# Recurrence of an RWKV-7 layer: head norms as 64x64 products, joined with other TensorE work, in a new order

## The reference, cut to what matters

```python
kk = heads(k * k_k)
kk = kk / jnp.maximum(jnp.sqrt(jnp.sum(kk * kk, axis=-1, keepdims=True)), 1e-12)
k = k * (1.0 + (a - 1.0) * k_a)
b_h = kk * a_h
def step(S, inp):
    r_t, w_t, k_t, v_t, na_t, b_t = inp
    sa = jnp.einsum('bhvk,bhk->bhv', S, na_t)
    S = S * w_t[:, :, None, :] + sa[..., None] * b_t[:, :, None, :] + v_t[..., None] * k_t[:, :, None, :]
    return S, jnp.einsum('bhvk,bhk->bhv', S, r_t)
...
mean = jnp.mean(out, axis=-1, keepdims=True)
var = jnp.mean(jnp.square(out - mean), axis=-1, keepdims=True)
out = ((out - mean) * lax.rsqrt(var + LNX_EPS)).reshape(B, T, D) * lnx_w + lnx_b
```

## Time and profile before

| | |
|---|---|
| median of 3 runs | 3540.37 us (3538.47 to 3543.31) |
| the profiled execution | 3546.33 us, its span 3544.6 us |
| granted TensorE clock, mean | 0.987 of full |
| TensorE busy | 3381.6 us of the span |
| VectorE, ScalarE, GpSimd busy | 1652.6, 1354.5, 1740.5 us |
| the recurrence, first product of decays to last of the states | 415.2 to 1126.4 us |

### The profile page before, as it was taken

The page is one execution under the profiler, slowest core; times in us unless marked ns, Lnnn a source line. Parts: engine busy times, 40 slices in busy tenths (PEclk is TensorE's granted clock), DMA queues, the critical chain, the costliest instruction groups (busy, mean ns, idle before and its releaser), DMA issues. The chain is left out here.

```text
span 3544.6 us, 87445 instructions
## 1 busy us (share of the span) xinstructions
PE 3381.6 (95%) x33525; PEld 2940.6 (83%) x33525; DVE 1652.6 (47%) x3032; ACT 1354.5 (38%) x2917; POOL 1740.5 (49%) x1622
## 2 busy tenths in 40 slices
PE   8999889998898999999999999999989999999999
PEld 8999778777777998888888887777769988888887
DVE  7113356555554374444444533333343744444444
ACT  6212445554443133333333434444453333333335
POOL 4434266666654445454554544344433354545455
PEclk9999899999999999999999999999999999999999
DMA  4422211111114011111111234444442111111111
GB/s 154 154 88 89 71 35 36 43 41 38 38 44 143 10 45 46 48 44 45 44 46 47 87 85 96 114 102 91 107 108 66 41 46 47 43 50 42 47 44 73
DMA packets 432743, 233.86 MB, mean 66 GB/s; under 512 B 190979, under 2 KB 417043, under 8 KB 431558
## 3 DMA queue, kind: packets, MB, share of 16 engines
q1 hardware_dynamic: 428882, 215.40, 21.9%
q10 hardware_dynamic: 3572, 14.33, 1.0%
HBM read 187.69 MB, written 47.21 MB: 66 GB/s over the span
## 5 line engine op out<-in xcount | busy, mean ns | idle before, releaser
L2688 DVE TENSOR_TENSOR H<-ps,H 128x512 f32<-128x512 f32 x608 | 419.6, 690 | 463.3 <-PE ps L2351 462.5
L2239 POOL TENSOR_TENSOR split<-work,split 128x512 fp32r<-128x512 f32 x280 | 379.8, 1361 | 493.9 <-ACT split L2510 486.8
L2351 PE MATMUL ps<-split,split 128*128 128x512 f32 x1824 | 514.0, 390 | 0.0
L2404 PE MATMUL ps<-xs,split 128*128 128x512 f32 x1920 | 512.5, 393 | 0.0
L1341 PE MATMUL ps<-arena 64*64 64x64 f32 (+1 forms) x9984 | 400.9, 225 | 37.9 <-issue 21.2
L1341 PEld LDWEIGHTS ps<-arena 64*64 64x64 f32 x9984 | 351.6, 135 | 71.4 <-issue 45.6
L2404 PEld LDWEIGHTS ps<-xs,split 128*128 128x128 f32 x1920 | 349.9, 188 | 68.2
L2351 PEld LDWEIGHTS ps<-split,split 128*128 128x128 f32 x1824 | 339.8, 188 | 70.9 <-DVE H L2688 0.7
L2404 PE MATMUL ps<-split,split 128*128 128x512 f32 x1440 | 366.1, 390 | 0.5 <-issue 0.5
L3278 PE MATMUL ps<-xs,split 128*128 128x384 f32 x1656 | 361.4, 355 | 2.6 <-POOL split L3192 2.6
L601 PE MATMUL ps<-mixed,wsplit_mix 128*128 128x384 f32 x1872 | 331.7, 339 | 7.6 <-DVE mixed L824 7.6
(11 more groups left out here) (325 smaller groups left out, 5972.4 us busy)
## 6 DMA issues: line engine op xcount, KB each, us to landing
work<-in_ffn_w_gu SPq DMA_DIRECT2D x168, 256.0 KB, 2.9
work<-in_ffn_w_down SPq DMA_DIRECT2D x168, 128.0 KB, 2.3
work<-in_cache_v SPq DMA_DIRECT2D x64, 256.0 KB, 3.9
work<-in_cache_k SPq DMA_DIRECT2D x256, 64.0 KB, 2.2
rkv_scratch<-lora ACTq DMA_DIRECT2D x24, 576.0 KB, 2.8
stage_mix<-in_rwkv_w_rkv SPq DMA_DIRECT2D x24, 512.0 KB, 3.8
work<-in_attn_w_qkv SPq DMA_DIRECT2D x24, 512.0 KB, 4.2
h_scratch<-H SPq DMA_DIRECT2D x2, 4608.0 KB, 12.5
```

The source lines that it names most:

```text
L2239: pool.tensor_tensor(w[1], frm, w[0].bitcast(F32), ALU.subtract).then_inc(u_lo, 1)
L2351: last = pe.matmul(full(DOWN + j % 2), w[part][:, (m % 2) * P:(m % 2 + 1) * P], mem.hid[xpart][:, SEG[h]], start=(a == 0), stop=(a == 2))
L2404: last = pe.matmul(full(to), unit(i)[part][:, k * P:(k + 1) * P], operand[xpart][:, k, :], start=(first and k == 0 and a == 0), stop=(k == ...
L2688: dve.tensor_tensor(at, full(DOWN + j % 2), at, ALU.add).then_inc(added, 1)
```

## The change

- `sums` and `expanded` are made of crossed 64x64 products: for each third (6 blocks of 64 columns) six `cross` calls, the sums with 16 columns of ones, the turned roots with the identity. `ksum` and `vsum` are now three items a pair instead of one, each with a turn of the piece bank, and VectorE thresholds each third; the reciprocal and the root still come once, after the third.
- `joined` gets a third case, "under": a piece of a norm next to a fold, or next to a first half of the inverse, is merged with it.
- `FIRST` and the first use of `PATTERN` are replaced by `START` (248 letters for the same items with the new thirds), and `PATTERN` is new (165 letters).
- In the last pair the thirds of `vsum` have their own banks.

```diff
-FIRST = (
-    "CCCCCCCCCCCCCCCCCCCCBBBCCCBCCCCBCCEBECBBEBCBCECFFBCFCCFCCFEBFCFCEBCCFCCCBEBEBFCECCFECFECCCE")
+START = (
+    "CCCCCCCCCCCCCCCCCCCCCCCCBBBCCBCCBECECBCEBBECEBFCCFCFCECFCFBBECCCEFCCEBFBAEFCCCCEECFBCCFAEAEFACCBEBAFBAAECFACAF"
+    "EBFBAECFCAEBFACECAFEBFBEAFACAEBCCBEACAABFBAECAFCCAAECACCBFCECFCACECAFEAEBFEACECCFCAFEBAECAEBFAECAFBECFBAAEACBF"
+    "AACAECAAFAEAABEAFCAAEAFECCAE")
 PATTERN = (
-    "EBADFBAEDABEAFDFEADAFBAEFAAECDADADBFECAFEACFBEBCFAEDAECCAABFAEADAECAFCEADABFCEABECACFAEACEAAEFCAFCAEECABABFAAA"
-    "EFACBEACAFBECCAACFACEBBFCAAEAFCEBBECAAEFCEAFEACFCCE")
+    "DEFADAAEFDAEDAFDEADACBFEBAFEDBADFADEBDAECBEACBEAFCCABEACFAAEAAFECAAEBFACCEBDFAECACFBCEAFACAEFACDAFECAECACBFBAF"
+    "EAEAAACEBABFEAAECCCFAAAECBFEBFCEAAABEAFBACEFACCEFCACECC")
...
+NORMS = ("ksum", "kexp", "vsum", "affine")
...
             out[-1] = ("beside", before[1], (before, key))
+        elif before and before[0] in NORMS and (key[0] == "fold" or key[0] == "invert" and key[2][2] == 0):
+            out[-1] = ("under", key[1], (key, before))
+        elif before and key[0] in NORMS and (before[0] == "fold" or before[0] == "invert" and before[2][2] == 0):
+            out[-1] = ("under", before[1], (before, key))
...
-    for o in range(PAIRS):
-        threads = {"A": serial_items(o) if o + 1 < PAIRS else last_serial_items(), "D": finish_items(o - 1) if o else []}
+    assert not rest.pop("A")
+    for o in range(1, PAIRS):
+        threads = {"A": serial_items(o) if o + 1 < PAIRS else last_serial_items(), "D": finish_items(o - 1)}
...
+            def sums(pb, squares, c, j):
+                return cross(pb[:, TS * j:TS * j + TS], squares[:, c * CW + 64 * j:c * CW + 64 * j + 64], mem.ones[:, 0:TS])
+
+            def expanded(pb, roots, c, j):
+                return cross(pb[:, 64 * j:64 * j + 64], roots[:, c * CW + 64 * j:c * CW + 64 * j + 64], None)
...
+                elif what == "under":
+                    (turn, _, inner), (norm, np, c) = arg
+                    g = inner if turn == "fold" else inner[0]
+                    G = GROUPS[g][1]
+                    if turn == "fold":
+                        fold_start(pr, g)
+                    else:
+                        level_start(pr, g, inner[1])
+                    norm_start(norm, np, c)
+                    for q in range(G):
+                        last = fold_part(g, q) if turn == "fold" else square(pr, g, inner[1], q)
+                        for j in range(6 * q // G, 6 * (q + 1) // G):
+                            norm_part(norm, np, c, j)
+                    last.then_inc(folded[LINE[g]] if turn == "fold" else m1_done[LINE[g]], 1)
...
                 elif what == "ksum":
-                    dve.tensor_scalar(roots(0), head_sums(pb), 1e-24, None, ALU.max).then_inc(piece_free[b], 1)
-                    dve.wait_ge(piece_free[b], n + 1)
-                    dve.reciprocal(m.rs[:, 0, :], m.rs[:, 0, :]).then_inc(kinv, 1)
+                    dve.tensor_scalar(roots(0, arg), head_sums(pb), 1e-24, None, ALU.max).then_inc(piece_free[b], 1)
+                    if arg == 2:
+                        dve.wait_ge(piece_free[b], n + 1)
+                        dve.reciprocal(m.rs[:, 0, :], m.rs[:, 0, :]).then_inc(kinv, 1)
```

More of the change, by code:

```diff
@@ L998, in prepare_items @@
         out += [("w", o, c), ("a", o, c), ("scan", o, c)]
-    out += [("ksum", o, None)] + [("decays", o, c) for c in range(3)]
+    out += [("ksum", o, c) for c in range(3)] + [("decays", o, c) for c in range(3)]
     out += [("kexp", o, c) for c in range(3)] + [("k2", o, None), ("b", o, None)] + [("write", o, g) for g in range(NG)]
@@ L1060, in recurrence_order @@
     for_tensor = list(out)
-    for c, after in enumerate((("vsum", o, None), ("affine", o, 2), ("nst", o, 0))):
+    for c, after in enumerate((("vsum", o, 2), ("affine", o, 2), ("nst", o, 0))):
         for_tensor.remove(("gate", o, c))
@@ L1348, in cross, with norm_start, norm_part @@
                 return last
[L1350 to L1361, removed]
+            def sums(pb, squares, c, j):
+                return cross(pb[:, TS * j:TS * j + TS], squares[:, c * CW + 64 * j:c * CW + 64 * j + 64], mem.ones[:, 0:TS])
+            def expanded(pb, roots, c, j):
+                return cross(pb[:, 64 * j:64 * j + 64], roots[:, c * CW + 64 * j:c * CW + 64 * j + 64], None)
+            def norm_start(what, pr, c):
+                b, n = PIECE_OF[what, pr, c]
+                if n:
+                    pe.wait_ge(piece_free[b], n)
+                if what == "ksum":
+                    pe.wait_ge(kq_ready, pr + 1)
+                elif what == "kexp":
+                    pe.wait_ge(kroot, pr + 1)
+                elif what == "vsum":
+                    cb, cn = PIECE_OF["center", pr, c]
+                    pe.wait_ge(piece_free[cb], cn + 1)
+                else:
+                    pe.wait_ge(vroot, pr + 1)
+            def norm_part(what, pr, c, j):
+                b, n = PIECE_OF[what, pr, c]
+                pb = bank[:, PIECE_BANKS[b], :]
+                if what in ("ksum", "vsum"):
+                    last = sums(pb, m.k2 if what == "ksum" else m.post1, c, j)
+                else:
+                    last = expanded(pb, m.kkn if what == "kexp" else m.post1, c, j)
+                if j == 5:
+                    last.then_inc(piece_done[b], 1)
             def state_values(n):
@@ L1463, in _ @@
                 e = pr % 2
-                if what in PIECES:
+                if what in PIECES and what not in ("ksum", "kexp", "vsum", "affine"):
                     b, n = PIECE_OF[key]
@@ L1474, in _ @@
                     last.then_inc(piece_done[b], 1)
[L1475 to L1478, removed]
-                    pe.wait_ge(kroot, pr + 1)
-                    expanded(pb, m.kkn, arg).then_inc(piece_done[b], 1)
+                elif what in ("ksum", "kexp", "vsum", "affine"):
+                    norm_start(what, pr, arg)
+                    for j in range(6):
+                        norm_part(what, pr, arg, j)
                 elif what == "rk":
@@ L1490, in _ @@
                     cross(pb[:, 0:CW], m.center, third(m.out, arg)).then_inc(piece_done[b], 1)
-                elif what == "vsum":
-                    for c in range(3) if pr == PAIRS - 1 else (2,):
-                        cb, cn = PIECE_OF["center", pr, c]
-                        pe.wait_ge(piece_free[cb], cn + 1)
-                    sums(pb, m.post1).then_inc(piece_done[b], 1)
-                elif what == "affine":
-                    pe.wait_ge(vroot, pr + 1)
-                    expanded(pb, m.post1, arg).then_inc(piece_done[b], 1)
                 elif what == "gate":
@@ L1691, in _ @@
                     act.copy(m.vb[:, e, c0:c0 + G, :], part(m.v)).then_inc(written_act, 1)
-                elif what == "ksum":
+                elif what == "ksum" and arg == 2:
                     if pr:
```

51 lines of the change are left out of this document (29 added, 22 removed).

## The result

The changed kernel takes 3591.16 us (median of 4 runs, 3587.22 to 3594.12) against 3539.63 us (3538.47 to 3543.31): the ratio is 1.0143, with an interval of 1.0126 to 1.0161. It is 51 us slower; the forecast was 34 us faster.

What follows compares the result with a forecast made beforehand. The prediction took TensorE's time to bound the kernel, with GpSimd's queue setting the pace in part of each pair. Terms -42 + 9 + 3.5 + 1 - 6 gave -34.5 us, a forecast of 3506 us, range 3480 to 3540.

Steps and rivals of the forecast that it cites:

- What bounds the kernel: Whole kernel: TensorE is busy 3381.6 of 3544.6 us, so taking away its busy or idle time pays.
- Removed in all: 78 us: Old norms in the recurrence: 16 sum calls at 2.44 us and 48 root items at 0.81 us disappear.
- The 0.3 us of emptying: Ahead of each old sum call and root item: about 0.3 us goes in emptying the array.
- What a piece costs: 96 new norm pieces: 41 under other work at 0.35 us, 55 alone at 0.50, together 41.9 us.
- Joined formings, -11.9 us: Formings joined with inverse second halves go from 95 to 112, each of the 17 saving 0.7 us.
- the issue bound: Rival on TensorE: each matmul costs its slot, so joins hide little; 3532 us, chance 0.15.
- Joined steps, +6: Steps joined with inverse first halves go from 17 to 76, each of the 59 costing 0.1 us.
- The coupled waits: Rival at the 59 new step joins: each waits for both halves; at 0.8 us each, 3553 us, chance 0.12.
- "What is not gained", +9 us: GpSimd's full stretch in each pair: 1.3 us of saved TensorE time turns into waiting, over seven pairs.
- The first pair: Its own order brings step 0 sooner and wins 6 of 17.5 us of TensorE idle time.
- my lower bound: Least gain allowed from the first pair's new order: 0 us, with 12 as the upper bound.
- the clock for the first pair (+3.5): First pair at low clock: six chained pieces of 1.4 us replace 4.0 us plus three short ones, adding 3.5 us.

Runs made afterwards that it cites:

- e17: Kernel before, sums as straight 64x64 products of 384 columns a third, roots as exp(-0.5 ln x) on ScalarE, no turned roots: 3589.63 us, 1.0114.
- e19: Kernel before, every matmul of the old sums and every transpose of the turned roots issued twice: 3583.79 us, 1.0121.
- e16: Kernel before, two of GpSimd's 1,152-column products cut to a third: 3540.12 us, 0.9986.
- e1: Changed kernel with the old order strings, keeping the new crossed norms and their joins: 3568.07 us, 1.0066 to the kernel before.
- e2: Kernel before with the new order strings, keeping the old whole-array sums and transposes: 3566.09 us, 1.0058.
- e14: Changed kernel without the 76 joins of steps with first halves: 3591.88 us, 1.0123 to the kernel before.
- e13: Changed kernel, writes of pairs 3 to 7 eight items earlier on VectorE and ScalarE, GpSimd's order kept: 3596.12 us, 1.0156 to the kernel before.
- e15: Changed kernel, two of GpSimd's 1,152-column products cut to a third: 3588.09 us, 1.0116 to the kernel before.
- e6: Kernel before with only the first pair's new order string, old pattern and norms kept: 3543.76 us, 1.0002.
- e7: Kernel before with empty TensorE instructions that never reached the chip, so the same program again: 3547.58 us, 1.0002.
- e10: Kernel before with two long-satisfied waits ahead of each straight and each crossed pair of TensorE products: 3687.95 us, 1.0416.

## Why the prediction was wrong

**What bounds the kernel.** "An edit pays if it takes TensorE time away" was the first wrong step. The change took 12 us of TensorE's work out and the phase grew by 47, for clock, block stops and waits are part of the price and had hardly a term. e17 took 49 us out and lost too, though there ScalarE's 41 us more are a cause of their own. Yet TensorE's time is not free: 47 us put in (e19) cost 26 to 43. That a chain through the other engines (masks, copies, W, states) sets the pair fits the waits, but no run shows which chain it is; e16 shows that it is not the amount of GpSimd's work.

**"Removed in all: 78 us"** is the first term of the sum that failed. The 0.3 us of emptying, credited 64 times, was read wrongly. Ahead of the sums at 782.69 the fold's last matmul starts at 782.49, and ahead of the calls, and of the thirds that wait for nothing, it is mostly 0.14 to 0.20 us from start to start, 0.11 to 0.17 more than a matmul's usual 29 ns. At 830.71 the last matmul starts at 830.29, but 0.20 us of that gap is the wait for VectorE that the row shows. So a call takes about 2.3 us and a third 0.60: 65 us in all. e17 agrees: 49 us of work less, and its own products, at the 0.30 us a third of its expectation, are 14. A second copy adds only 47 us, as it follows the first with no switch (2.01 us a call and 0.33 a third).

**What a piece costs** is the second: 0.44 us on average in the forecast, 0.55 to 0.65 in place. The durations of single pieces were nearly right. Standing alone for one piece of sums and then under a fold of two chunks for the next, in the kernel after:

```profile
981.63:982.24 0.61, 0.61 (x36) 0.61 (x32) 0.18 (x1) 0.37 (x1) 0.10 (x1) 1.00 0.58 219
982.97:983.70 0.73, 0.73 (x32) 0.73 (x34) 0.02 (x1) 0.04 (x1) 0.00 (x0) 1.00 0.91 292
```

0.61 where I took 0.50, and 0.73 for both. Under a first half of 16 matmuls it is 0.72 for both (674.99 to 675.71), where I expected 0.75. But in place the pieces cost more than the 42 us of the sum: a second copy adds 61 us of work (0.63 each), and the 65 us taken out left 12 to 13 with the new order and 2 with the old one (e1), so the pieces took about 52 and 63 us. That they take the overlap which their neighbours had at their seams would explain it, and is not shown. Two more things had no term: the new norms go with a lower clock, and their 48 instructions each use up a block sooner. So work fell by 12 us instead of 42: 13 us are the removed term, 10 or 11 the pieces, 6 the joins below.

**Joined formings, -11.9 us**: nothing of it is seen. e2 has 17 more of them and 59 more joined steps, and 546.2 us of work against 545.9, where I had -12 and +6. That part of the issue bound was right; its cause, a floor per matmul, is not shown. **Joined steps, +6**: taking the 76 joins away changes nothing beyond the intervals (e14). The coupled waits, my slower rival, priced 59 of them at 35 us and more and did not happen: the kernel is slower for other reasons.

**"What is not gained", +9 us**, had the right kind and the wrong place and size: waits grew by 24 us, as much as with the order alone (e2). I had looked for them in GpSimd's stretch. A large part is seen at the seam (the wait for W is 18.1 us; before, as the line below shows, it was 9.6), where k2, b and the writes of the next but one pair now stand right ahead of step 0; but e13 took that wait away and gained nothing. Which chain holds the pairs of the new order stays open. It isn't the amount of GpSimd's work (e15), nor the joins (e14), nor the place of VectorE's writes alone (e13).

```profile
PE ps L1347 <- DVE arena L1853: 9.6, 9, 2.0
```

**The first pair**: step 0 comes 8 us sooner (71.0 against 78.7), and pair 0 takes 16 us more; with the old norms the string alone is worth 0 (e6), my lower bound. I charged the clock for the first pair (+3.5) and nowhere else; outside it the changed kernel has some 30 us more at the lower level.

**Chances.** Slower had 0.12, and for a reason that did not happen. The range ended at 3540, as nearly all its terms were of TensorE's time; the clock outside the first pair and the block stops stood in none of the rivals.

## What to carry to other kernels

Before taking time out of a busy engine, measure what it costs in place: from the start of the matmul ahead to the start of the one behind, with waits taken off. The old norms were 65 us so, not 78. Doubling them in place costs one run and shows how much of such time counts (26 to 43 us of 47 here), but it leaves the switch into the item out. Count the instructions that an edit adds to the densest engine and read the granted clock beside its busy share: a wait of some 3 us on TensorE can be paid a second time as half speed behind it. And joining two items in the code gains little where neighbours already overlap.

## What was unexpected of the hardware

- TensorE stops at a fixed place of each 256 of its instructions when it has used 256 up in less than about 4 us: 43 us of stops in this phase before, 61 after, 8 to 14 where a block took longer.
- The granted clock fell to 0.50 five times in the steady pairs of the kernel after, for 3 to 7 us, 1.7 to 3.4 us lost each time; four of the falls came at TensorE's stops of 2.6 to 3.6 us from start to start at the seams, one behind shorter stops. With the new sums in the old order it fell too (e1, 27 us at the lower level there). What about them does it was not tried. Before, no steady pair had a fall, but in e7, the same program, three did, so a single profile does not settle this.
- Two satisfied waits ahead of a pair of products, one of them an instruction of its own, take 0.044 us of TensorE's time (e10).
- VectorE's reciprocal of 384 columns takes 2.55 us, 6.6 ns a column; that of 18 columns takes 0.27. The Trainium skill (VectorE: DVE Perf Modes, First, the fixed hardware budget) says that a reciprocal is an iterative divide with a repeat count of 8. The trace agrees as far as that a reciprocal is slow: a SCALAR_TENSOR_TENSOR of 384 columns takes 0.61 us in the kernel before, a quarter; it doesn't show the count.
